# Moving eight column units of the key/value modulation from beside the projections to beside layer 0's attention

## The chip, the cores and the metric

One core of one Trainium2 chip runs the whole program. The metric is the device time of one execution in microseconds. Five engines each run their own instruction list in order: PE (TensorE, matrix products), DVE (VectorE), ACT (ScalarE), POOL (GpSimd) and SP (SyncE), which here only issues the loads of the weights. They meet through semaphores.

## The reference

A decoder of two layers works on 256 tokens of width 1024. All numbers are 32-bit floats.

```
for layer in (0, 1):
    shift, scale, gate (twice each) = silu(c) @ w_ada[layer] + b_ada[layer]
    u = rmsnorm(h) * (1 + scale_m) + shift_m
    layer 0: mix = forgetting attention(u): q, k, v, log f = u @ w_in_a
             q, k = rmsnorm per head; p = softmax(q k / 8 + cum f_q - cum f_k, causal); mix = (p v) @ w_o_a
    layer 1: shared keys/values from rmsnorm(h), modulated by silu(c) @ w_ada_kv; three-branch attention
    h = h + gate_m * mix
    u = rmsnorm(h) * (1 + scale_f) + shift_f
    h = h + gate_f * (64 routed experts, top 8 of them per token, + one shared expert)(u)
```

Two parts matter here. Layer 0's projection has 12 units of 256 columns: four of queries, four of keys, four of values. The modulation vectors are products of one row, silu(c), with wide matrices. Vectors 2 to 7 (gate, and the shift, scale and gate of the feed-forward part of layer 0, and shift and scale of the key/value side) are the ones that the change touches.

## The kernel before

**The ring.** Every weight comes to the core as a unit of 1 MB. One list, `ring_order`, says in which order the units are loaded into 14 slots. SP walks it (L1397): unit n is issued when unit n - 14 has been used up. The list begins with 8 units of layer 0's first two modulation vectors; then come the 12 projection units, `("qkv", j)`, each followed by `COLS_OF_QKV[j]` column units, 24 in all; then eight later column units and the four units of the output projection, mixed; then the experts of layer 0. Numbered from 0, the last projection unit is unit 41, and the first expert unit is unit 56.

**A column unit** holds 256 output columns of a modulation matrix. PE has nothing to do with it: DVE multiplies it with the row silu(c), in two passes of 1024 elements per partition (`dve_columns`, L614), each of which sums into one column of `vectors`. `dve_vectors(done, 1, ...)` adds the biases once all 24 early units are read.

**The projections.** For each unit PE runs `pe_rows_unit` (L565: 16 products, each with two records in the trace) into one PSUM bank. For the eight query and key units ACT squares the result, DVE forms sums and norms the heads (`dve_head_norm`, L917 to L929), PE turns the normed rows (L1619) and ACT copies them to `qT` and `kT_a`. DVE takes its column units between the norms of unit after unit. The four value units are only copied by ACT (L1908) into `v_a`.

**The attention** of layer 0 has eight batches of four heads and 128 queries: four with 128 keys each (t = 0), then four with 256 (t = 1). For each batch, in order: PE computes logits (`pe_logits`, L692 and L697); DVE adds the mask, takes the maximum and negates it (`mask`, L792 to L796); ACT takes exponents (L775); PE turns the probabilities (`turn`, L716); ACT copies them (L767); PE multiplies with the values (`weigh`, L737); DVE divides (`output`, L803 and L2125). Each engine runs ahead by its own order. PE's for batch b is logits(b + 2), weigh(b - 1), turn(b). DVE's is

```
mask(0); mask(1)
for b in range(len(batches)):
    if beside: beside(b)
    if b + 2 < len(batches): mask(b + 2)
    if b >= 1: output(b - 1)
output(len(batches) - 1)
```

Layer 0 passes no `beside`; layer 1 does.

**After it** PE turns the heads (L474) and runs the output projection; DVE prepares the gate (L640), works out the rotary angles, reads two column units, then waits for the gate row (ACT L655), and then for each of three output units reads two more column units and adds the rows (L899, L901). The norm, the router and the choice of experts follow. SP needs the chosen order (`order_i`, waited for at L1419) to load any expert beyond the first four.

Of the kernel before, what the change touches and what calls it, by code (L numbers as in the profile page):

```python
# [24 lines left out]
ALU = mybir.AluOpType  # L25
ACT = mybir.ActivationFunctionType
# [5 lines left out]
NT = SEQ // P  # L32
# [14 lines left out]
QK_SCALE = DH ** -0.5  # L47
# [52 lines left out]
OF_LAYER = [0, 8]  # L100
# [8 lines left out]

VECTOR_STAGES = [range(0, 2), range(2, 8), range(8, 10), range(10, 12), range(12, VECTORS)]  # L110
COLS_PER_VECTOR = 4
COLS_OF_QKV = [2, 2, 1, 2, 1, 2, 1, 2, 3, 3, 3, 2]
COLS_OF_OUT = [2, 2, 2, 2]
COLS_OF_KV = [2, 2, 2, 1, 1]
COLS_OF_OUT_B = [6, 1, 1]
# [21 lines left out]
def ring_order():  # L137

    early, late, last, mixed = (iter(cols_of(i)) for i in range(1, 5))
    order = [("ada", j) for j in range(ADA_UNITS)]  # L140
    for j in range(12):
        order += [("qkv", j)] + [("cols", next(early)) for _ in range(COLS_OF_QKV[j])]
    for j in range(4):
        order += [("cols", next(late)) for _ in range(COLS_OF_OUT[j])] + [("out_a", j)]
    order += expert_units(0)
    for j in range(3):
        order += [("kv", j)] + [("cols", next(last)) for _ in range(COLS_OF_KV[j])]
    order += [("kv", 3)] + [("cmp", j) for j in range(4)] + [("cols", next(last)) for _ in range(COLS_OF_KV[3])]
    order += [("kv", 4), ("kv", 5)] + [("cmp", j) for j in range(4, 8)]
    order += [("cols", next(last)) for _ in range(COLS_OF_KV[4])]  # L150
    order += [("q", j) for j in range(4)]
    for j in range(3):
        order += [("cols", next(mixed)) for _ in range(COLS_OF_OUT_B[j])] + [("out_b", j)]
    order += [("out_b", 3)]
    return order + expert_units(1)
# [46 lines left out]
def build(nc, a, out):  # L202
    with ExitStack() as ctx:
# [5 lines left out]
        def sem(name):  # L209
            if name not in sems:  # L210
                sems[name] = ctx.enter_context(nc.semaphore(name))
            return sems[name]
# [219 lines left out]
        def bcast(ap, shape):  # L432
            return ap.to_broadcast(shape)


        ROUTING_SEMS = ["router_out", "router_copied", "router_turned", "scores_ready", "mask_ready", "ranks_out", "unranked_ready", "unranked_turned",
                        "unranked_copied", "place_ready", "ranked_out", "order_ready", "over_ready", "ends_out",
                        "items_ready", "items_out", "tables_ready", "shared_act", "shared_hid",
# [116 lines left out]
        def pe_rows_unit(pe_, n, bank, lhs, step_ready=None, between=None):  # L555

            landed(pe_, n)
            w = slot(n)
            for t in range(NT):
                if t and between:  # L560
                    between()
                for k in range(KC):
                    if step_ready and t == 0:
                        step_ready(k)
                    mm = pe_.matmul(PS[:, bank, t * UC:(t + 1) * UC], lhs[:, k, t * P:(t + 1) * P],  # L565
                                    w[:, k, :], start=(k == 0), stop=(k == KC - 1))
            mm.then_inc(unit_done, 1)
# [71 lines left out]
        def dve_gate_diag(done, i):  # L639
            done(done.eng.tensor_tensor(gate_diag, of_halves[:, :].unsqueeze(1).to_broadcast([P, KC, DH]),  # L640
                                        vectors[:, GATES[i], :].unsqueeze(2).to_broadcast([P, KC, DH]), ALU.mult),
                 gate_diag_ready)
# [37 lines left out]
        def pe_logits(pe_, kind, batches, keys, b):  # L680
            br, t, g = batches[b]
            w = width(t)
            if b >= 2:
                pe_.wait_ge(scores_read, BATCHES_FROM[kind] + b - 1)
            if kind == "nsa":
                pe_.wait_ge(sem("rotated_copied"), g + 1)
            o = logit_banks(b).rearrange("p (half pair) w -> p half pair w", half=2)
            for i in range(2):
                pair = 2 * g + i
                for half in range(2):  # L690
                    rows = slice(half * DH, (half + 1) * DH)
                    mm = pe_.matmul(o[:, half, i, 0:w], qT[rows, pair, t * P:(t + 1) * P],  # L692
                                    keys(br, pair)[rows, 0:w], start=True, stop=(kind != "fox"))
                if kind == "fox":
                    for half in range(2):
                        rows = slice(half * DH, (half + 1) * DH)
                        mm = pe_.matmul(o[:, half, i, 0:w], forget_queries[rows, t * P:(t + 1) * P],  # L697
                                        forget_keys[rows, pair, 0:w], start=False, stop=True)
            mm.then_inc(logits_out, 1)
# [119 lines left out]
        def act_table(act, function):  # L819
            act.activation(unused[:, :], eps_col[:, :], function)  # L820
# [754 lines left out]
        def _(pe_):  # L1575
# [35 lines left out]
            def turn_unit(j):  # L1611
# [8 lines left out]
                                           src[:, t, c * P:(c + 1) * P], ident[:, :])  # L1620
                mm.then_inc(sem("fox_turned"), 1)

            for j in range(12):
                if j == 11:
                    pe_.wait_ge(sem("fox_v"), 1)
                elif j >= 3:
                    pe_.wait_ge(sem("fox_normed"), j - 2)
                pe_rows_unit(pe_, AT["qkv", j], j % 3, uT)
                if 1 <= j <= 8:
                    turn_unit(j - 1)  # L1630
                if j == 0:
                    forget_turn()
                elif j == 2:
                    forget_sums()
                elif j == 3:
                    forget_turn_rows()
            pe_.wait_ge(forget_rows, 5)
            pe_.wait_ge(sem("fox_copied"), 8)
            pe_.wait_ge(sem("fox_v"), 4)

            def fox_keys(br, pair):
                return kT_a[:, pair, :]

            for b in range(2):
                pe_logits(pe_, "fox", fox_batches, fox_keys, b)
            pe_attention(pe_, "fox", fox_batches, fox_keys,
                         lambda br, kt, hd: v_a[:, kt, hd, :])
            pe_turn_rows(pe_, u, (heads_read, 8), "fox_o")
# [223 lines left out]
        def _(act):  # L1872
# [33 lines left out]
            for j in range(4):  # L1906
                used_up(act, ("qkv", 8 + j))
                done(act.activation(v_a[:, :, 4 * j:4 * j + 4, 0:DH],  # L1908
                                    PS[:, (8 + j) % 3, :].rearrange("p (t h d) -> p t h d", t=NT, h=4), ACT.Copy),
                     sem("fox_v"))  # L1910
                if j == 0:
                    copy_unit(7)
            act_table(act, ACT.Exp)
            act_attention(done, "fox", fox_batches)
            act_copy_turned(done, uT, "fox_o")
            act.wait_ge(sem("angles"), 2)
# [116 lines left out]
        def _(dve):  # L2033
# [42 lines left out]
            for j in range(12):  # L2076
# [7 lines left out]
                if j < 8:  # L2084
                    if j >= 2:
# [1 line left out]
                    dve_head_norm(done, "foxn", j, j % 3,  # L2087
                                  normed[j % 2].rearrange("p (t h d) -> p t h d", t=NT, h=4),
                                  (gain_qa if j < 4 else gain_ka)[:, :], sem("fox_normed"))
            dve.wait_ge(params, 16 * N_PARAMS)  # L2090
            done(dve.tensor_scalar(gain_qb[:, :], gain_qb[:, :], QK_SCALE, None, ALU.mult))
            dve_vectors(done, 1, [(OF_LAYER[0] + SC_F, 1), (OF_KV + 1, 2)])

            def rope_angles():
                dve.wait_ge(consts, 1)
# [29 lines left out]
                done(dve.tensor_tensor(u[:, t, g * UC:(g + 1) * UC].rearrange("p (i d) -> p i d", i=4), heads,  # L2125
                                       rinv.unsqueeze(2).to_broadcast([P, 4, DH]), ALU.mult), heads_read)

            dve_attention(done, "fox", fox_batches, fox_finish)

            def add_mix(layer, name, beside=None):  # L2130
                dve.wait_ge(gate_ready, 2 * layer + 1)
# [22 lines left out]
                dve_columns(dve, [next(late) for _ in range(COLS_OF_OUT[j])])  # L2154

            dve_gate_diag(done, 0)
            rope_angles()
            columns_of_out(0)
            add_mix(0, "out_a", lambda j: columns_of_out(j + 1))
# [252 lines left out]
```

## Time and profile before

| what | us |
|---|---|
| median of 3 runs | 1393.42 (1393.15 to 1394.42) |
| the profiled execution, its own time | 1396.53 |
| its span, first to last instruction | 1394.8 |
| PE busy, of the span | 1338.6 (96%) |
| DVE busy | 428.8 (31%) |
| DMA, bytes and mean rate | 512.94 MB, 368 GB/s |

The busy shares are means over stages with different limits: layer 0's projections and attention fill the time up to about 160 us, its output projection and routing the time up to about 219 us, its experts the time to about 790 us, then layer 1 in the same order. "PE busy" counts matmul records with modelled ends.

### The profile page before, as it was taken

The numbers are of one execution on the slowest core, as the hardware profiler recorded it, in microseconds if no ns is written. First come the engines' busy times: TensorE is split into PE (matmuls) and PEld (weight loads), VectorE is DVE, ScalarE is ACT, GpSimd is POOL, SyncE is SP. The second block draws the span as 40 slices with busy tenths as digits, with TensorE's granted clock in tenths as the row PEclk, the third lists the DMA queues.
The fourth block names the chain that finished last, engine by engine and source line by source line (L and its number), as shares of the span: only waits on it lengthen the run. The fifth ranks groups of instructions, "written<-read, shape, count | busy, mean of one in ns | idle before, by whom it ended". The sixth has DMA issues, their size and how long they took to land.

```text
span 1394.8 us, 20069 instructions
## 1 busy us (share of the span) xinstructions
PE 1338.6 (96%) x8011; PEld 783.8 (56%) x8011; DVE 428.8 (31%) x969; ACT 268.4 (19%) x534; POOL 32.1 (2%) x82
## 2 busy tenths in 40 slices
PE   5998989999999999999899899899999999999997
PEld 1887865465444444444388788754564444444442
DVE  1799672101111111111183698611111111111111
ACT  2222531110111111011133563410110111111100
POOL 4000000001000000000000000000010000000000
PEclk9999999999999999999999999999999999999999
DMA  9999666999999999999999602579999999999996
GB/s 381 390 421 421 266 247 260 385 421 361 423 420 421 422 421 421 421 421 421 421 417 420 252 1 90 220 307 383 420 362 422 420 421 422 421 421 422 420 421 286
DMA packets 71774, 512.94 MB, mean 368 GB/s; under 512 B 8240, under 2 KB 8448, under 8 KB 9728
## 3 DMA queue, kind: packets, MB, share of 16 engines
q1 hardware_dynamic: 70560, 509.64, 88.6%
q0 software_dynamic: 832, 1.39, 0.5%
q8 instruction: 65, 1.06, 0.3%
q10 hardware_dynamic: 288, 0.61, 0.1%
q14 instruction: 29, 0.24, 0.0%
HBM read 510.55 MB, written 1.05 MB: 367 GB/s over the span
## 4 chain that ended last, share of the span: by engine, by line
PE 80%; DMA 8%; DVE 7%; ACT 2%; issue 2%; SPq 1%; DVEq 0%; ACTq 0%
PE PS L987 24%; PE PS L977 13%; PE PS L995 12%; PE PS L1011 11%; PE PS L565 6%; DMA ring<-in_w_in_a_units 4%; DMA ring<-in_w_exp 4%; DVE ring L614 2%; PE PS L737 2%; PE PS L1023 2%; SPq L1397 1%; PE PS L692 1%; PE PS L1852 1%; PE PS L1032 1%; PE PS L716 1%
## 5 line engine op out<-in xcount | busy, mean ns | idle before, releaser
L987 PE MATMUL PS<-ring,scratch 128*32 128x512 f32 (+2 forms) x2176 | 353.7, 593 | 6.7 <-DMA ring<-in_w_exp 5.3
L987 PEld LDWEIGHTS PS<-ring,scratch 128*32 128x32 f32 (+2 forms) x2176 | 111.0, 122 | 242.3 <-issue 240.6
L1342 DVE TENSOR_TENSOR scratch<-PS,gate_row 128x512 f32<-128x512 f32 x100 | 69.2, 692 | 462.3 <-PE PS L995 462.3
L977 PEld LDWEIGHTS PS<-scratch,u 128*128 128x128 f32 x1600 | 186.2, 194 | 38.4 <-issue 36.5
L977 PE MATMUL PS<-scratch,u 128*128 128x128 f32 x1600 | 195.4, 281 | 1.4 <-ACT scratch L1206 1.4
L995 PE MATMUL PS<-ring,scratch 128*32 128x512 f32 (+2 forms) x1088 | 182.2, 596 | 3.4 <-DMA ring<-in_w_exp 2.2
L1011 PE MATMUL PS<-scratch 128*128 128x512 f32 x384 | 172.7, 592 | 0.0
L565 PE MATMUL PS<-ring,uT 128*128 128x256 f32 x672 | 148.6, 380 | 3.6 <-DMA ring<-in_w_in_a_units 3.4
L1214 ACT ACTIVATE scratch<-PS 128x256 f32<-128x256 f32 x50 | 19.2, 384 | 672.9 <-PE PS L987 672.9
L565 PEld LDWEIGHTS PS<-ring,uT 128*128 128x128 f32 x672 | 126.3, 190 | 22.6 <-issue 4.2
L1330 DVE TENSOR_TENSOR scratch<-scratch,PS 128x256 f32<-128x256 f32 x50 | 21.1, 422 | 329.7 <-ACT scratch L1214 329.7
L995 PEld LDWEIGHTS PS<-ring,scratch 128*32 128x32 f32 (+2 forms) x1088 | 52.8, 122 | 123.3 <-issue 121.6
L614 DVE SCALAR_TENSOR_TENSOR ring<-ring,cond_row 128x1024 f32<-128x1024 f32 x96 | 111.8, 1220 | 4.8 <-ACT gate_row L655 3.9
L1011 PEld LDWEIGHTS PS<-scratch 128*128 128x128 f32 x384 | 69.2, 190 | 68.9 <-issue 68.9
L1206 ACT ACTIVATE scratch<-PS 128x512 f32<-128x512 f32 x100 | 59.7, 597 | 145.7 <-PE PS L977 145.7
L737 PE MATMUL PS<-scratch,uT 128*128 128x65 f32 x288 | 37.0, 279 | 4.7 <-ACT uT L767 4.4
L737 PEld LDWEIGHTS PS<-scratch,uT 128*128 128x128 f32 x288 | 34.6, 195 | 9.1 <-issue 6.4
L775 ACT ACTIVATE scratch<-scratch,stats 128x128 f32<-128x128 f32 (+1 forms) x96 | 35.6, 444 | 11.9 <-DVE stats L796 11.9
L1219 ACT ACTIVATE scratch<-PS 128x512 f32<-128x512 f32 x50 | 29.6, 592 | 2.7 <-PE PS L1005 2.7
L565 PE MATMUL PS<-ring,u 128*128 128x256 f32 x128 | 28.7, 381 | 0.0
L1023 PE MATMUL PS<-uT,ring 128*128 128x256 f32 x128 | 28.3, 379 | 0.0
L1023 PEld LDWEIGHTS PS<-uT,ring 128*128 128x128 f32 x128 | 24.3, 190 | 5.0 <-issue 1.9
(346 smaller groups left out, 856.9 us busy)
## 6 DMA issues: line engine op xcount, KB each, us to landing
ring<-in_w_exp SPq DMA_DIRECT2D x384, 1024.0 KB, 16.4
ring<-in_w_ada_columns SPq DMA_DIRECT2D x48, 1024.0 KB, 25.6
ring<-in_w_in_a_units SPq DMA_DIRECT2D x12, 1024.0 KB, 27.5
ring<-in_w_ada_units SPq DMA_DIRECT2D x8, 1024.0 KB, 16.1
ring<-in_w_cmp_units SPq DMA_DIRECT2D x8, 1024.0 KB, 24.0
ring<-in_w_sh_units SPq DMA_DIRECT2D x6, 1024.0 KB, 13.7
ring<-in_w_kv_b_units SPq DMA_DIRECT2D x6, 1024.0 KB, 22.4
ring<-in_w_o_a_units SPq DMA_DIRECT2D x4, 1024.0 KB, 26.4
```

The costliest lines, as they stand in the source:

```text
L565: mm = pe_.matmul(PS[:, bank, t * UC:(t + 1) * UC], lhs[:, k, t * P:(t + 1) * P], w[:, k, :], start=(k == 0), stop=(k == KC - 1))
L614: ins = dve.scalar_tensor_tensor(out=w[:, c, :], in0=w[:, c, :], scalar=1.0, in1=cond_row[:, :], op0=ALU.mult, op1=ALU.mult, accum_out=vec ...
L737: mm = pe_.matmul(PS[:, heads_bank(kind, b), hd * (DH + 1):(hd + 1) * (DH + 1)], pT[:, n * P:(n + 1) * P], values(br, kt, 4 * g + hd), sta ...
L775: eng.activation(p, p, ACT.Exp, bias=stats[:, b % 3, 4 + i:5 + i]).then_inc(probs_ready, 1)
L977: mm = pe_.matmul(PS[:, bank, i * w:(i + 1) * w], u[:, t, k * P:(k + 1) * P], hot[:, t, :], start=(t == 0), stop=(t == NT - 1))
L987: mm = pe_.matmul(PS[places, GU, :], x[:, kk, places], gate_and_up, start=(kk == 0), stop=(kk == KC - 1))
L995: mm = pe_.matmul(PS[places, Y0 + half, :], hT[:, j, places], down[:, j, half * 512:(half + 1) * 512], start=(j == 0), stop=(j == 1))
L1011: mm = pe_.matmul(OUT[t][:, half * 512:(half + 1) * 512], hot_wT[0:rows, t * P:(t + 1) * P], y_rows[0:rows, half * 512:(half + 1) * 512], ...
L1023: mm = pe_.matmul(PS[:, GATHER, i * SEQ:(i + 1) * SEQ], slot(AT[unit])[:, k, i * P:(i + 1) * P], uT[:, k, :], start=(k == 0), stop=(k == K ...
L1206: act.activation(x_pair[g % 2][:, 4 * half:4 * half + 4, :].rearrange("p k s -> p (k s)"), PS[:, gather_bank(g, half), :], ACT.Copy).then_ ...
L1219: act.activation(turned_sb[g % 2], PS[:, GU, :], ACT.Copy).then_inc(group_sem["turned_copied"], 1)
L1342: dve.tensor_tensor(y_rows[:, half * 512:(half + 1) * 512], PS[:, Y0 + half, :], gate_row[:, half * 512:(half + 1) * 512], ALU.mult).then_ ...
```

## The change

Eight of the 24 early column units leave the projections and go behind the last projection unit in the ring; DVE reads one of them at the start of each attention batch, ahead of `mask(b + 2)` (`columns_of_fox`, handed over as `beside`). The last projection unit becomes unit 34 of the ring. `dve_vectors(done, 1, ...)` moves behind the attention, and the scaling of `gain_qb` behind the gate's preparation. On PE the logits of batch 0 are issued ahead of the last value unit, those of batch 1 behind it; the value units go to banks 2, 6, 7, 6 so that the logits' banks 0 and 1 are free, with the waits that this needs. ACT loads its table for exponents ahead of the last value copy instead of behind it.

```diff
--- before.py
+++ after.py
@@ -109,7 +109,8 @@
 
 VECTOR_STAGES = [range(0, 2), range(2, 8), range(8, 10), range(10, 12), range(12, VECTORS)]
 COLS_PER_VECTOR = 4
-COLS_OF_QKV = [2, 2, 1, 2, 1, 2, 1, 2, 3, 3, 3, 2]
+COLS_OF_QKV = [2, 2, 1, 1, 1, 1, 1, 1, 1, 2, 2, 1]
+COLS_BESIDE_FOX = 8
 COLS_OF_OUT = [2, 2, 2, 2]
 COLS_OF_KV = [2, 2, 2, 1, 1]
 COLS_OF_OUT_B = [6, 1, 1]
@@ -140,6 +141,7 @@
     order = [("ada", j) for j in range(ADA_UNITS)]
     for j in range(12):
         order += [("qkv", j)] + [("cols", next(early)) for _ in range(COLS_OF_QKV[j])]
+    order += [("cols", next(early)) for _ in range(COLS_BESIDE_FOX)]
     for j in range(4):
         order += [("cols", next(late)) for _ in range(COLS_OF_OUT[j])] + [("out_a", j)]
     order += expert_units(0)
@@ -433,6 +435,7 @@
             return ap.to_broadcast(shape)
 
 
+        V_BANK = [2, 6, 7, 6]
         ROUTING_SEMS = ["router_out", "router_copied", "router_turned", "scores_ready", "mask_ready", "ranks_out", "unranked_ready", "unranked_turned",
                         "unranked_copied", "place_ready", "ranked_out", "order_ready", "over_ready", "ends_out",
                         "items_ready", "items_out", "tables_ready", "shared_act", "shared_hid",
@@ -1620,12 +1623,20 @@
                                            src[:, t, c * P:(c + 1) * P], ident[:, :])
                 mm.then_inc(sem("fox_turned"), 1)
 
+            def fox_keys(br, pair):
+                return kT_a[:, pair, :]
+
             for j in range(12):
-                if j == 11:
-                    pe_.wait_ge(sem("fox_v"), 1)
-                elif j >= 3:
+                if j == 9:
+                    pe_.wait_ge(forget_rows, 5)
+                elif j == 11:
+                    pe_.wait_ge(sem("fox_copied"), 8)
+                    pe_.wait_ge(sem("fox_normed"), 8)
+                    pe_logits(pe_, "fox", fox_batches, fox_keys, 0)
+                    pe_.wait_ge(sem("fox_v"), 2)
+                elif 3 <= j <= 8:
                     pe_.wait_ge(sem("fox_normed"), j - 2)
-                pe_rows_unit(pe_, AT["qkv", j], j % 3, uT)
+                pe_rows_unit(pe_, AT["qkv", j], V_BANK[j - 8] if j >= 8 else j % 3, uT)
                 if 1 <= j <= 8:
                     turn_unit(j - 1)
                 if j == 0:
@@ -1634,15 +1645,8 @@
                     forget_sums()
                 elif j == 3:
                     forget_turn_rows()
-            pe_.wait_ge(forget_rows, 5)
-            pe_.wait_ge(sem("fox_copied"), 8)
+            pe_logits(pe_, "fox", fox_batches, fox_keys, 1)
             pe_.wait_ge(sem("fox_v"), 4)
-
-            def fox_keys(br, pair):
-                return kT_a[:, pair, :]
-
-            for b in range(2):
-                pe_logits(pe_, "fox", fox_batches, fox_keys, b)
             pe_attention(pe_, "fox", fox_batches, fox_keys,
                          lambda br, kt, hd: v_a[:, kt, hd, :])
             pe_turn_rows(pe_, u, (heads_read, 8), "fox_o")
@@ -1906,11 +1910,12 @@
             for j in range(4):
                 used_up(act, ("qkv", 8 + j))
                 done(act.activation(v_a[:, :, 4 * j:4 * j + 4, 0:DH],
-                                    PS[:, (8 + j) % 3, :].rearrange("p (t h d) -> p t h d", t=NT, h=4), ACT.Copy),
+                                    PS[:, V_BANK[j], :].rearrange("p (t h d) -> p t h d", t=NT, h=4), ACT.Copy),
                      sem("fox_v"))
                 if j == 0:
                     copy_unit(7)
-            act_table(act, ACT.Exp)
+                elif j == 2:
+                    act_table(act, ACT.Exp)
             act_attention(done, "fox", fox_batches)
             act_copy_turned(done, uT, "fox_o")
             act.wait_ge(sem("angles"), 2)
@@ -2087,9 +2092,8 @@
                     dve_head_norm(done, "foxn", j, j % 3,
                                   normed[j % 2].rearrange("p (t h d) -> p t h d", t=NT, h=4),
                                   (gain_qa if j < 4 else gain_ka)[:, :], sem("fox_normed"))
-            dve.wait_ge(params, 16 * N_PARAMS)
-            done(dve.tensor_scalar(gain_qb[:, :], gain_qb[:, :], QK_SCALE, None, ALU.mult))
-            dve_vectors(done, 1, [(OF_LAYER[0] + SC_F, 1), (OF_KV + 1, 2)])
+            def columns_of_fox(b):
+                dve_columns(dve, [next(early) for _ in range(COLS_BESIDE_FOX // len(fox_batches))])
 
             def rope_angles():
                 dve.wait_ge(consts, 1)
@@ -2125,7 +2129,8 @@
                 done(dve.tensor_tensor(u[:, t, g * UC:(g + 1) * UC].rearrange("p (i d) -> p i d", i=4), heads,
                                        rinv.unsqueeze(2).to_broadcast([P, 4, DH]), ALU.mult), heads_read)
 
-            dve_attention(done, "fox", fox_batches, fox_finish)
+            dve_attention(done, "fox", fox_batches, fox_finish, columns_of_fox)
+            dve_vectors(done, 1, [(OF_LAYER[0] + SC_F, 1), (OF_KV + 1, 2)])
 
             def add_mix(layer, name, beside=None):
                 dve.wait_ge(gate_ready, 2 * layer + 1)
@@ -2154,6 +2159,8 @@
                 dve_columns(dve, [next(late) for _ in range(COLS_OF_OUT[j])])
 
             dve_gate_diag(done, 0)
+            dve.wait_ge(params, 16 * N_PARAMS)
+            done(dve.tensor_scalar(gain_qb[:, :], gain_qb[:, :], QK_SCALE, None, ALU.mult))
             rope_angles()
             columns_of_out(0)
             add_mix(0, "out_a", lambda j: columns_of_out(j + 1))
```

## Rows read from the trace of the kernel before

**Rows 1.** The page, the span in 40 equal slices of 34.87 us, clock and DMA in tenths.
```profile
PEclk9999999999999999999999999999999999999999
DMA  9999666999999999999999602579999999999996
```

**Rows 2.** Timeline, PE, the last projection units: start, us, engine, operation, idle before.
```profile
103.56 13.98 PE L565 MATMUL PS<-ring,uT 128*128 128x256 f32 x64
...
119.39 7.14 PE L565 MATMUL PS<-ring,uT 128*128 128x256 f32 x32 [1.85 <-DMA ring<-in_w_in_a_units]
```

**Rows 3.** Busy time by windows: window, length, each engine, clock, DMA share, GB/s.
```profile
90.00:98.00 8.00, 8.00 (x41) 7.05 (x40) 7.39 (x16) 1.40 (x3) 0.00 (x0) 1.00 1.01 421
...
128.00:160.00 32.00, 29.46 (x266) 25.04 (x263) 21.37 (x41) 18.94 (x46) 0.00 (x0) 1.00 0.90 373
```

**Rows 4.** Timeline, DVE: first passes of two column units that follow each other.
```profile
101.97 1.22 DVE L614 SCALAR_TENSOR_TENSOR ring<-ring,cond_row 128x1024 f32<-128x1024 f32 x1
...
104.27 1.22 DVE L614 SCALAR_TENSOR_TENSOR ring<-ring,cond_row 128x1024 f32<-128x1024 f32 x1
```

**Rows 5.** Timeline of the attention's start, PE, DVE and ACT.
```profile
127.38 0.49 PE L692 MATMUL PS<-scratch 64*128 64x128 f32 x4 [0.84 <-ACT scratch L1908]
...
128.34 0.42 PE L692 MATMUL PS<-scratch 64*128 64x128 f32 x4
...
128.64 0.69 DVE L792 TENSOR_TENSOR scratch<-PS,causal 128x512 f32<-128x512 f32 x1 [0.63 <-PE PS L697]
...
130.29 0.69 DVE L792 TENSOR_TENSOR scratch<-PS,causal 128x512 f32<-128x512 f32 x1
130.29 1.28 ACT L775 ACTIVATE scratch<-scratch,stats 128x128 f32<-128x128 f32 x4 [1.55 <-DVE stats L796]
```

**Rows 6.** Timeline, DVE: one mask with t = 1, one output, the next mask.
```profile
137.33 1.22 DVE L792 TENSOR_TENSOR scratch<-PS,causal 128x1024 f32<-128x1024 f32 x1 [1.45 <-PE PS L697]
...
140.05 0.18 DVE L803 RECIPROCAL stats<-PS 128x4 f32<-128x4 f32 x1
...
140.74 1.22 DVE L792 TENSOR_TENSOR scratch<-PS,causal 128x1024 f32<-128x1024 f32 x1
```

**Rows 7.** Timeline, from the last batch's turning to the gate row.
```profile
156.03 1.04 PE L716 MATMUL PS<-ident,scratch 128*128 128x128 f32 x8
...
156.68 1.09 ACT L767 ACTIVATE uT<-PS 128x512 f32<-128x512 f32 x2 [2.10 <-PE PS L716]
157.42 1.97 PE L737 MATMUL PS<-scratch,uT 128*128 128x65 f32 x16 [0.34 <-ACT uT L767]
...
159.71 0.42 DVE L2125 TENSOR_TENSOR u<-PS,stats 128x256 f32<-128x256 f32 x1
160.17 0.69 DVE L640 TENSOR_TENSOR scratch<-of_halves,vectors 128x512 f32<-128x512 f32 x1
160.19 3.60 PE L474 MATMUL PS<-ident,u 128*128 128x128 f32 x16 [0.80 <-DVE u L2125]
...
164.35 1.23 DVE L614 SCALAR_TENSOR_TENSOR ring<-ring,cond_row 128x1024 f32<-128x1024 f32 x1
...
172.92 1.22 DVE L614 SCALAR_TENSOR_TENSOR ring<-ring,cond_row 128x1024 f32<-128x1024 f32 x1 [3.89 <-ACT gate_row L655]
```

**Rows 8.** Windows of 4 us, columns as in Rows 3: where the clock fell, and where not.
```profile
160.00:164.00 4.00, 3.81 (x18) 3.79 (x19) 3.45 (x17) 1.91 (x4) 0.00 (x0) 0.57 0.02 4
...
208.00:212.00 4.00, 3.55 (x21) 3.23 (x21) 2.87 (x12) 0.83 (x2) 0.00 (x0) 0.50 0.00 0
...
844.00:848.00 4.00, 2.80 (x26) 2.59 (x25) 3.77 (x7) 2.62 (x7) 0.00 (x0) 1.00 0.00 0
```

**Rows 9.** A window in the routing, SP's wait for the order, SP's next load.
```profile
204.00:208.00 4.00, 1.27 (x9) 0.59 (x6) 2.35 (x11) 3.92 (x4) 0.00 (x0) 0.99 0.00 0
...
SPq L1419 <- DVE order_i L1301: 56.4, 2, 29.1
...
219.81 1.34 SPq L1397 DMA_DIRECT2D ring<-in_w_exp  x2
```

## The prediction

> **What bounds the kernel now.** I read four views in this order.
>
> First the slices of the page [rows 1]. They show that the DMA engines are full nearly throughout, but fall to 6 tenths in slices 5 to 7 (139 to 244 us) and to nothing around slice 24. A pause of the DMA is where something other than the weights sets the time. The edits fall into slices 1 to 5, up to the first pause.
>
> Second the timeline of PE through the projections [rows 2]. The reader is to see that the units follow without a gap: units 9 and 10 of the projection together take 103.56 to 117.54, 6.99 each, and only unit 11 waits, 1.85 us, for its weights. The window from 90 to 98 us says the same, PE 8.00 of 8.00 while DVE has 7.39 and the DMA runs at 421 GB/s [rows 3]. So two things run nearly level here, but PE is the one that sets the pace, with 1.85 us of DMA on top at the end.
>
> Third the attention, 128 to 160 us. PE is busy for 29.46 us of 32, DVE for 21.37 [rows 3]. DVE has 10.63 us free. The chain of waits goes around from PE to DVE to ACT and back; DVE waits for PE in most batches (1.45 us before the mask that starts at 137.33 [rows 6]).
>
> Fourth what follows. After the attention DVE is done with its first two late column units about 4 us before the gate row comes (it idles 3.89 us [rows 7]), and from there the routing is a plain chain. In the routing the DMA moves nothing, and SP stands at L1419 for the order of the experts, 29.1 us at the longest; its next load goes out at 219.81 [rows 9]. A shift of the attention's end is therefore a shift of the routing, of that load and of all that comes after. Nothing behind it has slack that would absorb it: the loads that the chosen order gates cannot start sooner, and PE starts on the experts from the same routing.
>
> **The change, part by part.**
>
> *Fewer column units among the projections.* Seven fewer stand ahead of projection unit 11 in the ring (41 becomes 34). A unit of 1.049 MB at 421 GB/s takes 2.49 us [rows 3], so its weights come up to 17 us sooner. But only the wait can be saved: 1.85 us. PE cannot start unit 11 before unit 10 ends, 117.54 [rows 2]. DVE's free time in that stretch buys nothing, as PE had no gap to close. The waits before the second and third unit stay, as the column units ahead of those are the same.
>
> *Logits of batch 0 ahead of unit 11.* One batch of them takes 0.96 us of PE (127.38 to 128.34 [rows 5]). Queries and keys are complete by then: unit 8 and the last turn are over at 103.56 [rows 2], and the last key copy follows directly. Unit 11 then starts at 118.50 and ends at 118.50 + 7.14 = 125.64 (before: 119.39 + 7.14 = 126.53). That is 0.89 us sooner.
>
> *The start of the attention.* Before, the first mask starts 1.26 us after the first logits (127.38 to 128.64) and the second at 130.29, so a mask with t = 0 takes 1.65 us [rows 5]. In the changed kernel mask(0) is done while unit 11 runs. Logits 1 need no value copy and can start at 125.64, so mask(1) starts at 125.64 + 1.26 = 126.90, where it was 130.29: 3.39 us sooner. Exponents 0 (1.28 us of ACT [rows 5]) still stand behind the copy of the last values in ACT's queue, which costs nothing, since DVE is what is late next (below).
>
> *Eight column units beside the batches.* This is the big term. Two column units that follow each other start 2.30 us apart (101.97 and 104.27 [rows 4]), so eight cost DVE 18.4 us. None of them can be read during unit 11: `beside(0)` stands behind mask(1), and mask(1) waits for logits that come after unit 11. DVE's list from mask(1) to the end:
>
> - masks with t = 0: number 1, 2 and 3, 3 x 1.65 = 4.95 us;
> - masks with t = 1: four, each 2.72 us (137.33 to 140.05 [rows 6]), 10.88 us;
> - outputs: seven at 0.69 us (140.05 to 140.74 [rows 6]), and the last at 0.60, 5.43 us;
> - column units: 18.4 us.
>
> The sum is 39.66 us. Before, the same stretch lasted from 130.29 to 160.13 [rows 5, 7], 29.84 us, and held 21.26 us of DVE work. So the columns use up 8.6 us of idle time and 9.82 us are left over. Could DVE still wait inside? PE was busy for 29.46 us with all eight batches [rows 3]; one with t = 1 is at most twice one with t = 0, so at most 4.9 us, while DVE needs 2.30 + 2.72 + 0.69 = 5.71. PE runs ahead. At the tail, mask(7) ends near 159.2. Its exponents take at most twice the 1.28 us of 128 keys [rows 5], and from its turning to the end of its weighing it was 3.36 us (156.03 to 159.39 [rows 7]): 165.1. DVE comes to the last output at 165.9. So I take no idle time. Attention ends at 126.90 + 39.66 = 166.56 instead of 160.13: **+6.43 us**.
>
> *Work put behind the attention.* The three vector instructions of `dve_vectors` and the scaling of `gain_qb` now stand there. DVE did the gate's preparation and 16 small instructions in 164.35 - 160.17 = 4.18 us [rows 7]; without the 0.72 or so of the first, whose row has 0.69, that is 0.22 us each, so four cost 0.87 us. They lie inside the idle 3.89 us ahead of the gate row: 0. Without that cover they would cost 0.9. The gate product of PE waits for about 0.7 us of them, but stands behind a whole output unit of some 7 us.
>
> *The queue of SP.* The eight units are numbers 36 to 43, and free the slots of 50 to 57. With batches of 4 to 5.7 us, the last output unit (55) is issued when batch 5 has read number 41, near 156 us, and lands well ahead of its use, which is behind three other units' products. The first two expert units (56, 57) go out near 161 and 164, where they went out by about 130; the ten behind them follow the late columns, as before. All twelve have until about 225 us, and the DMA is empty from some 200 us on (0.00 in 204 to 208 [rows 9]). Two loads later by 30 us are 5 us of DMA time moved into that gap: 0. Without the gap they would cost those 5 us.
>
> *Sum:* -3.39 + 9.82 + 0 + 0 = +6.43 us on the profiled execution (span 1394.8, own time 1396.53). Its own time stands 3.1 us above the median; I put the difference on the median: 1393.42 + 6.43 = **1399.9 us**, +0.46%.
>
> **Bounds.** TensorE's clock is the unknown. At the attention's end it is granted at 0.57 between 160 and 164 us and 0.50 between 208 and 212 [rows 8], so at 1.2 GHz in part or whole, and the turning of the heads took 3.60 us [rows 7]. If the new timing kept it at 2.4 GHz there, turning would take half (-1.8 us) and the second spot might give the same again: the lower bound is 6.43 - 3.6 = +2.8. If the lower level instead lasts on into the first output unit, up to half of that unit's 7.14 us doubles: +3.6, upper bound +10. Between them I keep the middle, as the clock fell before at a tail like the one expected.
>
> The Trainium skill ("TensorE: Matmul & The Clock Gate", section "What's actually happening") says that the throttled state is the default and that activity releases it. That rule speaks against this change, as it thins PE out: by it the next rival would be likelier. The trace agrees only in part, for the window of 844 to 848 had PE busy for 2.80 us of 4 at a clock of 1.00 [rows 8].
>
> **Rivals.**
>
> *The lower clock takes the attention.* PE's share falls from 29.46/32 = 0.92 to about 29.46/40 = 0.74 in the attention. If the clock went to 1.2 GHz, a batch would need up to 2 x 4.9 = 9.8 us of PE where DVE needs 5.71, 4.1 us more; two or three such batches give +8.2 to +12.3 us on top: 1408 to 1412 us. For it: the fall at 160 us. Against it: layer 1's attention, which shows 0.70 (2.80 of 4) beside a DVE at 3.77, keeps 1.00 there [rows 8]. Chance 0.10.
>
> *The shift is hidden.* If the weights' stream set the end by itself, the time of the routing would not matter, and the result is 1393.4, at most 0.9 less. For it: the DMA stands at 9 tenths in most slices [rows 1]. Against: it is empty for some 20 us before 219.81, and SP waits for the routing there [rows 9]. Chance 0.05.
>
> *Faster: the columns fit in the gaps.* If the column passes ran only in DVE's idle time, the attention would keep its pace and end 3.4 us sooner: 1390.0 us. It is decided by the price of one unit: the list has 21.26 us besides the columns and 166.56 becomes 160.13 when eight cost 160.13 - 126.90 - 21.26 = 11.97 us, 1.50 us each. Below 1.50 it is a gain, and at 1.07 the whole 3.4 (8.58 us of idle time by eight). The row has 2.30 [rows 4]; the passes touch only SBUF and have the same operands. Chance 0.05.
>
> **How the numbers follow.** DVE-bound attention, 1396.2 to 1403.5: 0.80. The rivals: 0.10, 0.05, 0.05. The likeliest is 1399.9. The range of 1396.2 to 1404 leaves out the rivals, 0.20 together. 0.2% is 2.8 us, about what a measurement can tell from no change. Faster by more than that: 0.05. Within it: the hidden shift and the lowest edge of the main case, 0.07. Slower: 0.88.
>
> **What the profile would show.** Unit 11 without a wait, its last record near 125.6; the second mask near 126.9; DVE without idle time between the masks, at 4.6 and 5.7 us per batch, where PE and ACT wait for it; the last output near 166.6; SP's load behind the routing near 226.2; and all later stages of the same length. A DVE that idles in the attention, a clock under 1.00 before 160 us, or a routing that does not shift would make the prediction wrong. So would a column pass that is not 1.22 us beside ACT and PE at work on the same PSUM and scratch.

## The result, and the profile after

The changed kernel takes 1407.2 us (median of 9 runs, 1401.19 to 1419.07), the kernel before 1394.42 (9 runs, 1391.8 to 1402.75). The ratio is 1.0094, 95% interval 1.0072 to 1.0116: slower by about 13 us, where 6.4 were forecast, and over the upper end of the forecast range (1404). The profiled execution of the changed kernel is its slowest run (1419.07 us, span 1417.3), so of its trace the places count, and the medians for the size.

The page, clock and DMA in 40 slices of 35.4 us (before: [rows 1]):

```profile
PEclk9999697999999999999999988999999999999999
DMA  9999474899999999999999700759999999999996
```

The clock has new holes in slices 5 and 7 and in slices 24 and 25. The last two lie in layer 1 (815 to 886 us), which the change does not touch.

Timeline of the changed kernel, from the last value unit on (before: [rows 2] and [rows 5]; L565 is now L568, L792 L795, L614 L617):

```profile
118.14 7.17 PE L568 MATMUL PS<-ring,uT 128*128 128x256 f32 x32
...
126.52 0.69 DVE L795 TENSOR_TENSOR scratch<-PS,causal 128x512 f32<-128x512 f32 x1 [6.65 <-PE PS L700]
...
128.17 1.23 DVE L617 SCALAR_TENSOR_TENSOR ring<-ring,cond_row 128x1024 f32<-128x1024 f32 x1
...
136.73 1.23 DVE L617 SCALAR_TENSOR_TENSOR ring<-ring,cond_row 128x1024 f32<-128x1024 f32 x1
...
142.41 1.22 DVE L617 SCALAR_TENSOR_TENSOR ring<-ring,cond_row 128x1024 f32<-128x1024 f32 x1
```

Unit 11 starts without a wait and is over at 125.3. The second mask starts at 126.52 (forecast: 126.90; the places of one and the same work differ by up to 0.9 us between profiled executions, so this gap says nothing). From there DVE shows no idle time, and a batch with 256 keys takes it 142.41 - 136.73 = 5.68 us (forecast: 5.71). Up to here the arithmetic held.

The same timeline, the tail (before: [rows 7]):

```profile
158.88 1.91 PE L719 MATMUL PS<-ident,scratch 128*128 128x128 f32 x8
...
161.12 3.65 PE L740 MATMUL PS<-scratch,uT 128*128 128x65 f32 x16 [0.34 <-ACT uT L770]
164.56 1.91 PE L719 MATMUL PS<-ident,scratch 128*128 128x128 f32 x8
...
165.03 0.42 DVE L2129 TENSOR_TENSOR u<-PS,stats 128x256 f32<-128x256 f32 x1
...
166.40 3.65 PE L740 MATMUL PS<-scratch,uT 128*128 128x65 f32 x16
...
170.16 0.18 DVE L806 RECIPROCAL stats<-PS 128x4 f32<-128x4 f32 x1 [4.71 <-PE PS L740]
...
170.85 3.68 PE L477 MATMUL PS<-ident,u 128*128 128x128 f32 x16 [0.80 <-DVE u L2129]
```

DVE has done output 6 by 165.45 and then waits 4.71 us for PE. Weighing takes PE 3.65 us where it took 1.97 before, and turning 1.91 instead of 1.04 [rows 7]. Two weighings and one turning stand in a row there: PE's list has the weighing of batch 6 ahead of the turning of batch 7. The attention ends at 170.79, not at 166.56.

Windows of 4 us of the changed kernel (columns as in [rows 3]):

```profile
140.00:144.00 4.00, 2.00 (x16) 1.46 (x16) 3.83 (x8) 2.19 (x5) 0.00 (x0) 1.00 0.91 348
144.00:148.00 4.00, 3.93 (x22) 3.46 (x24) 3.86 (x7) 0.58 (x2) 0.00 (x0) 0.60 0.58 190
...
152.00:156.00 4.00, 1.16 (x9) 0.95 (x8) 3.86 (x7) 2.67 (x6) 0.00 (x0) 0.88 0.56 231
156.00:160.00 4.00, 4.00 (x21) 4.00 (x21) 3.83 (x8) 1.21 (x3) 0.00 (x0) 0.50 0.68 238
...
168.00:172.00 4.00, 3.20 (x16) 3.01 (x16) 1.67 (x6) 0.00 (x0) 0.00 (x0) 0.50 0.24 102
...
224.00:228.00 4.00, 4.00 (x20) 3.42 (x20) 0.22 (x1) 0.60 (x1) 0.00 (x0) 0.50 0.01 2
```

PE has 2.00 of 4 us to do, then 1.16 of 4, while DVE is full; after each of them the clock is lower, and from 156 to 172 us it stands at 1.2 GHz.

How the shift grows along the program, in the two profiled executions, each number the start in the changed kernel less that before: turning of the heads 170.85 - 160.19 = 10.7 us; SP's first load of a chosen expert 231.48 - 219.81 = 11.7; SP's first load of the shared expert, deep in layer 0's experts, 288.53 - 272.70 = 15.8; the same load in layer 1, 988.63 - 966.25 = 22.4. The step from 11.7 to 15.8 has the lower clock beside it: it stood at 0.50 from 220 to 236 us in the changed kernel, over the end of the routing and the first expert products, and at 1.00 from 216 us on in the kernel before. The last step, 6.6 us, falls in layer 1, where the clock of this one execution was down for longer (slices 24 and 25).

### The profile page after: what moved, and what is told of

Same layout as the page of the kernel before. It is cut to its first block, busy times and chain, and to the rows that moved or that the text cites. A ratio compares the mean times of both kernels' runs of the same rounds, so it can differ in the third digit from the quotient of the medians.

```text
span 1417.3 us, 20074 instructions
## 1 busy us (share of the span) xinstructions
PE 1358.9 (96%) x8011; PEld 800.6 (56%) x8011; DVE 429.3 (30%) x969; ACT 268.3 (19%) x534; POOL 32.1 (2%) x82
## 3 DMA queue, kind: packets, MB, share of 16 engines
HBM read 510.55 MB, written 1.05 MB: 361 GB/s over the span
## 4 chain that ended last, share of the span: by engine, by line
PE 83%; DMA 6%; DVE 6%; ACT 2%; issue 1%; SPq 1%; DVEq 0%; ACTq 0%
PE PS L990 24%; PE PS L980 13%; PE PS L998 12%; PE PS L1014 11%; PE PS L568 10%; DMA ring<-in_w_exp 4%; DMA ring<-in_w_in_a_units 2%; PE PS L1026 2%; DVE ring L617 2%; PE PS L740 2%; SPq L1400 1%; PE PS L1856 1%; PE PS L1035 1%; PE PS L719 1%; DVE stats L798 1%
## 5 line engine op out<-in xcount | busy, mean ns | idle before, releaser
L568 PE MATMUL PS<-ring,uT 128*128 128x256 f32 x672 | 149.2, 381 | 1.2 <-DMA ring<-in_w_in_a_units 0.9
L568 PEld LDWEIGHTS PS<-ring,uT 128*128 128x128 f32 x672 | 126.8, 191 | 20.1 <-issue 1.9
L617 DVE SCALAR_TENSOR_TENSOR ring<-ring,cond_row 128x1024 f32<-128x1024 f32 x96 | 112.3, 1221 | 4.6 <-ACT gate_row L658 3.7
L740 PE MATMUL PS<-scratch,uT 128*128 128x65 f32 x288 | 44.0, 312 | 10.1 <-ACT uT L770 9.8
L740 PEld LDWEIGHTS PS<-scratch,uT 128*128 128x128 f32 x288 | 41.5, 227 | 15.1 <-issue 12.8
L568 PE MATMUL PS<-ring,u 128*128 128x256 f32 x128 | 28.7, 381 | 0.0
## 6 DMA issues: line engine op xcount, KB each, us to landing
ring<-in_w_kv_b_units SPq DMA_DIRECT2D x6, 1024.0 KB, 22.4
```

The lines of the kernel that those rows point to most:

```text
L617: ins = dve.scalar_tensor_tensor(out=w[:, c, :], in0=w[:, c, :], scalar=1.0, in1=cond_row[:, :], op0=ALU.mult, op1=ALU.mult, accum_out=vec ...
L740: mm = pe_.matmul(PS[:, heads_bank(kind, b), hd * (DH + 1):(hd + 1) * (DH + 1)], pT[:, n * P:(n + 1) * P], values(br, kt, 4 * g + hd), sta ...
```

## The experiments

Each is compared with the kernel before, run beside it in three groups (e1 to e4: median 1394.02; e5 to e8: 1393.94; e9 to e11: 1395.2; beside the changed kernel it had 1394.42). So times of different groups compare to about 1 us. "First shared load" is SP's first `w_sh` load in layer 0, a landmark free of layer 1; the kernel before has it at 272.70 us.

**e1: fill PE's idle time in the attention.** On the changed kernel:

```diff
+        BUSY_BEFORE_FOX_HEADS = {2: 4, 3: 8, 4: 8, 5: 8, 6: 8, 7: 8}
...
+                elif kind == "fox" and b in BUSY_BEFORE_FOX_HEADS:
+                    pe_keep_busy(pe_, BUSY_BEFORE_FOX_HEADS[b], heads_bank(kind, b), slice(4 * (DH + 1), 512 - P))
```

> The changed kernel with matrix products of no use put ahead of the weighing of the attention's batches 2 to 7 on PE (4, then 8 each, into unread columns of the heads' bank), so that PE does not fall idle there. Theory 1 (the excess over my forecast is TensorE's lower clock in the attention, its tail and what follows): the clock stays at 1.00 from 140 to 175 us, the last output comes near 166.5 us instead of 170.8, the output unit after it starts some 5 us sooner, and the median falls from 1407 to 1399 to 1401, with less spread. Theory 2 (the excess is DVE's or the ring's, or lies in layer 1): no change, 1405 to 1409, or slower by the added PE work.

Measured: 1401.59 us (12 runs, eleven of them 1400.59 to 1403.18), ratio 1.0049 (1.0032 to 1.0066). The clock is 1.00 through the attention, and turning the heads takes 1.97 us. The attention ends at 168.9, the first shared load comes at 278.39, 5.7 us after that of before. The chain that ended last shows why the end is not at 166.5 (start, us, what; L883 is the filling):

```profile
159.99 2.05 PE PS L883 x16
162.04 1.74 PE PS L742 x16
163.77 0.88 PE PS L719 x8
164.66 1.78 PE PS L883 x16
166.44 1.75 PE PS L742 x16
```

In the tail the filling stands in the chain itself, some 2 us. Even so the median is 5.6 us under that of the changed kernel, with more work to do. Theory 2 is out.

**e2: the columns alone.** The kernel before with the ring's order, `columns_of_fox` and the place of `dve_vectors` of the change, and nothing on PE or ACT:

```diff
+COLS_OF_QKV = [2, 2, 1, 1, 1, 1, 1, 1, 1, 2, 2, 1]
+COLS_BESIDE_FOX = 8
...
-            dve_attention(done, "fox", fox_batches, fox_finish)
+            dve_attention(done, "fox", fox_batches, fox_finish, columns_of_fox)
```

> The kernel before with the column units moved alone: PE, ACT and the banks as before, no logits ahead of the last value unit. Theory 1 (DVE sets the attention's pace, and the clock falls with it): the attention starts 1.8 us sooner than before, mask(1) near 128.5 us, so it ends some 2 us later than in the changed kernel; 1408 to 1411. Theory 2 (the harm comes from the reordered PE work, not from the columns): 1393 to 1396.

Measured: 1408.22 us (6 runs), ratio 1.0075 (1.005 to 1.0101). The turning of the heads starts at 172.70, 1.9 us after that of the changed kernel. The columns do the harm.

**e3: the first logits alone.** The changed kernel with `COLS_OF_QKV` as before and none beside the attention.

> The changed kernel with all 24 early column units beside the projections as before, so only the logits of batch 0, the banks, the table load and the place of the vector work are changed. Theory 1: DVE is full to 127.2 us with columns, so mask(0) comes at 127.2 instead of 128.6 and the gain is 1 to 1.5 us: 1392 to 1393.5. Theory 2 (the reordering itself does harm): above 1396.

Measured: 1393.87 us (12 runs), ratio 0.9992 (0.9972 to 1.0011). The turning starts at 158.67 (before 160.19), the first shared load at 271.77: about 1 us, as Theory 1 has it, and too small for the medians (1393.87 is just over its range).

**e4: two column units, in the tail.** The changed kernel with

```diff
+COLS_OF_QKV = [2, 2, 1, 2, 1, 2, 1, 2, 3, 3, 2, 1]
+COLS_BESIDE_FOX = [0, 0, 0, 0, 0, 0, 1, 1]
```

> The changed kernel with 22 column units beside the projections and only two beside the attention, at batches 6 and 7, where DVE of the kernel before waited 1.8 to 2.6 us for PE at each output. Theory 1 (columns cost only where DVE has no idle time left): the wait for unit 11 is gone, DVE is free for mask(0) at 123, no cost at the tail; attention ends near 157, 3 us sooner than before, and the clock falls no earlier than it did: 1389.5 to 1391.5. Theory 2 (any column unit in the attention thins PE out and costs the clock): 1396 or more.

Measured: 1394.91 us (12 runs, 1391.19 to 1400.48), ratio 1.0004 (0.9982 to 1.0027). The turning starts at 157.09 and the first shared load comes at 269.53, 3.2 us ahead of before, as expected; the median shows none of it. Four of the twelve runs are at 1400, with mean clocks of 0.983 to 0.985, while the fastest has 0.993. The places were predicted right and the time was not.

**e5: less filling, none in the tail.** As e1, with `{2: 4, 3: 6, 4: 6, 5: 6}`.

> The changed kernel with fewer of the idle-filling products than in the run with them ahead of batches 2 to 7: only ahead of the weighing of batches 2 to 5 (4, 6, 6, 6), none in the tail, where they delayed the last output by about 2.4 us. Theory 1 (my term of +6.4 us for DVE is right, the rest is the clock): the clock is 1.00 up to 158 us, the last output ends at 166 to 167 us, and the median is 1399.5 to 1400.5, 6 us over the kernel before. Theory 2 (the column units cost more than DVE's time): the last output stays at 168.5 or later and the median at 1401.5 or more.

Measured: 1411.7 us (5 runs, 1409.02 to 1413.07), ratio 1.012 (1.0093 to 1.0146). Theory 1 missed. The numbers of Theory 2 hold, but not its cause: DVE is done at 165.7 as forecast, and the last output's reciprocal starts at 169.00 after 3.33 us of waiting for PE. The clock was 0.88 from 160 to 164 us and 0.50 from there to 172. The filling that ended with batch 5 left the tail to the lower clock. Why the five runs lie 4.5 us above those of the changed kernel is not shown: the profiled one turns the heads at 169.70, sooner than the changed kernel, and it falls a further 3.9 us behind the kernel before only between 683 and 723 us, where layer 1 begins.

**e6: no column passes.** The changed kernel with the eight units waited for and freed, and two elements copied in place of the two passes.

> The changed kernel without the two passes over each of the eight column units beside the attention: DVE waits for the unit, copies two elements and frees the slot, so vectors 6 and 7 hold other values (key/value side of layer 1). It shows what the passes alone cost. Theory 1: DVE has 18 us less, the attention runs at the pace of PE and ACT as before, the clock stays up to its tail, and the last output ends near 157 us instead of 170.8; SP issues the first chosen expert near 217 us instead of 231.5; median 1389 to 1392. Theory 2 (the ring's order or the waits of PE do the harm): the attention still ends after 160.

Since vectors 6 and 7 feed layer 1, its median (1490.08 us) tells nothing; up to the end of layer 0 the trace can be read. The turning of the heads starts at 156.59 and takes 1.97 us; the first expert product comes at 213.47, where it came at 218.68 before and 232.07 in the changed kernel; the clock is 1.00 in every window from 118 to 200 us. The last output is where Theory 1 put it, and the first chosen load comes at 214.61, sooner than the 217 expected. The ring's order and PE's new waits cost nothing.

**e7: the kernel before with filling alone.** Ahead of the weighing of batches 6 and 7 one product each, three ahead of the turning, two in the routing:

```diff
+            pe_keep_busy(pe_, 3, 7, slice(4 * (DH + 1), 512 - P))
             pe_turn_rows(pe_, u, (heads_read, 8), "fox_o")
...
+            pe_keep_busy(pe_, 2, 7)
             pe_.wait_ge(routing["mask_ready"], layer + 1)
```

> The kernel before with idle-filling products alone: one ahead of the weighing of batches 6 and 7, three ahead of the turning of the heads, two of 512 columns in the routing ahead of the wait for the mask of chosen experts, where PE idles 2.7 us. Theory 1 (the clock is worth microseconds in the kernel before too, and its spread from 1391 to 1405 is the clock): turning takes 2.0 us instead of 3.6, the gather in the routing 2.0 instead of 3.6, 3 us less: 1390.5 to 1392, and fewer runs above 1398. Theory 2: no difference, since the clock falls elsewhere or by chance.

Measured: 1390.93 us (12 runs, 1389.24 to 1396.84), ratio 0.998 (0.9964 to 0.9995). Its timeline on PE:

```profile
159.75 1.97 PE L474 MATMUL PS<-ident,u 128*128 128x128 f32 x16
...
209.38 2.02 PE L980 MATMUL PS<-scratch,u 128*128 128x128 f32 x16
```

The turning took 3.60 before [rows 7]. The first shared load comes 3.2 us sooner. So the kernel before loses some 3 us to the clock too, and e7 does not get all of it back: its clock fell in another place of the routing (below, at e11).

**e8: e4 with the filling of e7.**

> The version with the first logits ahead and only two column units beside the attention, in its tail, with the same idle-filling products as in the run on the kernel before. Its attention ended 3.1 us sooner but its runs split between 1392 and 1400 us. Theory 1 (the split is the clock in the tail and the routing): 1387.5 to 1389.5 and fewer runs near 1400. Theory 2 (the split comes from layer 1, which nothing here touches): the low runs fall by 2 to 3 us, the share of high ones stays.

Measured: 1387.69 us (12 runs, 1385.37 to 1394.94), ratio 0.9952 (0.9934 to 0.9971): faster than both kernels. The turning starts at 156.53, the first expert product at 210.70, the first shared load at 264.73, 8.0 us ahead of before. Nine of the twelve runs are under 1390; the others, up to 1394.94, have mean clocks of 0.989 to 0.993.

**e9: filling in measure.** As e1, with `{2: 4, 3: 8, 4: 8, 5: 8, 6: 4, 7: 3}`.

> The changed kernel with idle-filling products ahead of the weighing of batches 2 to 7 (4, 8, 8, 8, then only 4 and 3 in the tail, where eight each had stood in the chain themselves). Theory 1 (DVE's list is the +6.4 us and the clock the rest): the clock stays at 1.00 to the end of the attention, the last output ends at 166.5 to 167.5 us instead of 168.9, and the median is 1399 to 1401. Theory 2 (the tail falls to the lower clock with so few): last output at 169 or later, median over 1404.

Measured: 1406.19 us (11 runs, 1401.55 to 1414.31), ratio 1.0074 (1.0048 to 1.0099). In the profiled execution the clock fell again, and the last output waited 4.92 us for PE, as Theory 2 had it. Five of the runs, up to 1403.05, lie where those of e1 do, the other six at 1406.19 and above. So e9 cannot tell how long DVE alone is, and e11 was made to.

**e10: four column units, batches 4 to 7.** As e4, with

```diff
+COLS_OF_QKV = [2, 2, 1, 2, 1, 2, 1, 1, 2, 2, 2, 2]
+COLS_BESIDE_FOX = [0, 0, 0, 0, 1, 1, 1, 1]
```

> First logits ahead, 20 column units beside the projections, four beside the attention, at batches 4 to 7. DVE's list after the first logits is 39.66 - 9.2 = 30.5 us. Theory 1 (the columns cost only what exceeds DVE's idle time): last output ends at 157.0 to 157.6 us, as with two units (157.0), median 1393 to 1395.5. Theory 2 (each unit costs in proportion, 1.2 us or so): the last output ends near 160, median 1397 or more.

Measured: 1402.62 us (12 runs, 1395.25 to 1407.81), ratio 1.0051 (1.0027 to 1.0076). Timeline:

```profile
158.62 0.18 DVE L806 RECIPROCAL stats<-PS 128x4 f32<-128x4 f32 x1
163.82 0.18 DVE L806 RECIPROCAL stats<-PS 128x4 f32<-128x4 f32 x1 [4.57 <-PE PS L740]
```

Output 6 comes at 158.62, later than the whole attention should have ended. Two things that the expectation left out bring it there: the second mask starts at 128.04, not at 126.9, and DVE still waits 1.56 us for PE before the mask that starts at 135.19, ahead of its first column unit, time that the units behind it cannot use. DVE's sum over the stage was too coarse. The last output then waits 4.57 us at the lower clock (0.50 in 156 to 168). Half the columns cost 7.4 us, where all of them cost 12.8. Theory 1 is out; Theory 2 has the median in its open range, but the last output, at 164.5, not near 160, and not the cause.

**e11: the changed kernel with the clock held.** The filling of e9, and three products ahead of the turning and two in the routing as in e7.

> The changed kernel with the even filling of the attention, three products ahead of the turning of the heads and two in the routing, the same as in the run on the kernel before that gave 1390.93. With the clock held in both, the difference is the change without the clock. Theory 1: DVE's list, +6.4 us, and up to 1 us of filling: 1397 to 1398.5. Theory 2 (the columns cost more than DVE's time, or the ring is late): 1400 or more.

Measured: 1397.27 us (12 runs, 1395.97 to 1398.4). Against e7, the kernel before with the same two fillings behind the attention, that is +6.34 us; their first shared loads, 276.15 and 269.53, are 6.62 apart. Timeline and two windows:

```profile
161.88 2.00 PE L742 MATMUL PS<-scratch,uT 128*128 128x65 f32 x16 [0.39 <-ACT uT L773]
...
165.26 1.90 PE L742 MATMUL PS<-scratch,uT 128*128 128x65 f32 x16
...
167.27 0.18 DVE L809 RECIPROCAL stats<-PS 128x4 f32<-128x4 f32 x1 [1.05 <-PE PS L742]
```

```profile
160.00:164.00 4.00, 3.28 (x27) 3.09 (x28) 3.90 (x8) 2.31 (x6) 0.00 (x0) 1.00 0.50 158
164.00:168.00 4.00, 3.92 (x36) 3.73 (x34) 2.84 (x9) 1.09 (x2) 0.00 (x0) 1.00 0.88 313
```

The attention ends at 167.9, 1.05 us of it a wait for PE. Its runs spread over 2.4 us, those of the changed kernel over 18.

The two landmarks are not a clean price of DVE's work. The attention of e11 ends at 167.90 and that of e7 at 159.69, 8.2 us apart. Of these, 1.05 are the wait for PE, and 0.85 stand in e11's trace before its attention begins (its first mask starts at 119.11, that of the changed kernel, with the same instructions up to there, at 118.25), which leaves 6.3. The shift is 1.6 us smaller behind the routing because e7's clock fell there, and its router products took 3.80 us where those of e11 took 2.22. Window and timeline of e7, then timeline of e11:

```profile
196.00:200.00 4.00, 3.71 (x23) 2.74 (x21) 2.84 (x7) 1.94 (x4) 0.00 (x0) 0.65 0.11 44
...
197.06 3.80 PE L534 MATMUL PS<-uT,scratch 128*64 128x256 f32 x16 [0.29 <-DMA scratch<-in_w_router_rows]
...
205.26 2.22 PE L537 MATMUL PS<-uT,scratch 128*64 128x256 f32 x16 [0.29 <-DMA scratch<-in_w_router_rows]
```

## Why the prediction was wrong

**The direction and the DVE sum were right.** DVE sets the pace of the changed attention, gap-free, at the forecast period. From the second mask on it has 39.5 us of work (126.52 to 165.45, and the last output), and the sum gave 39.66. With most of the clock's falls filled on both sides the change costs 6.34 us (e11 less e7), and the sum gave 6.43. That these two agree to 0.1 us is luck: each against the kernel before of its own group they are 5.1 us apart, and in the traces a wait for PE, a later start and e7's slower router products happen to cancel. That the weights' wait before unit 11 was all there was to win among the projections, that the ring has room, and that the routing carries the shift on, held too (e3, e6, the landmarks).

**The step that failed is the bound on TensorE's clock.** The prediction took the fall at the tail to be the same in both kernels ("Between them I keep the middle, as the clock fell before at a tail like the one expected"), took no idle time for DVE at the last output, put the clock's possible cost at +3.6 us at most, in the output unit alone, and gave the clock inside the attention a chance of 0.10. It is worth 1407.2 - 1397.3 = 9.9 us in the changed kernel (e11) and 1394.0 - 1390.9 = 3.1 us in the one before (e7). The difference, 6.8 us, stands beside the 6.34 of DVE, and together they are 13.1 where 12.8 were measured. Taken each against its own group the shares are 7.7 and 5.1. Both splits have to add up, being made of the same medians, so the sum is no test of its own; what shows the cause is that products of no use on PE alone took 9.9 us away. The prediction had named the signs: the clock was under 1.00 before 160 us (0.60 from 144 to 148), DVE waited 4.71 us, and SP's load behind the routing came at 231.48, not 226.2.

**Where it goes.** Not where the rival had it. Inside the batches the lower clock is hidden, as DVE is slower still: its period stays 5.68 us with PE at 1.2 GHz. The cost comes where DVE's masks run out, and one weighing, one turning and another weighing follow each other at 3.65, 1.91 and 3.65 us: the attention ends 4.2 us after its forecast in the profiled execution. The tail estimate had the last batch's steps without the batch ahead in PE's queue, and at the full clock; even with the clock held, the last output waits 1.05 us (e11, with 0.83 us of filling in it). More comes at the end of the routing and in the first expert products: the shift grows from 11.7 to 15.8 us between the first chosen load and the first shared one in the profiled executions. That the attention's thinner load also makes the later falls more frequent was not shown: e7 and e11 changed both places together.

**The rule against the change was weighed too low.** The Trainium skill ("TensorE: Matmul & The Clock Gate", "What's actually happening") has it that activity releases the throttle. The prediction set one window of layer 1 against it, PE busy 2.80 of 4 us at 1.00 [rows 8]. The changed kernel comes to 2.00 and 1.16 of 4, and there the trace agrees with the rule. The mean share that the prediction used (0.74) hid those windows. The busy share of one window does not decide it, though: in the kernel before PE was busy for 2.15 of 4 us from 116 to 120, and the clock stayed at 1.00 there and after.

**The rival "faster"** is out at the price in its own condition: a unit costs 2.30 us as before. It holds in part for two units in the tail (e4, e8), where DVE had idle time of that size.

## What to carry to other kernels

Work that is put beside a stage paced by round trips between engines costs first what exceeds its engine's idle time, batch by batch and in the order of the queue, and second what it takes from TensorE's load; here the second was about as large as the first. So count the other engine's period, then look at PE's busy share in the emptiest windows, as a warning and not as a rule, and price the tail at 1.2 GHz. Column work goes where DVE waits for PE anyhow, and short idle gaps on PE ahead of critical products are worth filling with products of no use, if the filling ends before the wait does.

## What the hardware showed that I had not expected

The clock's fall is not settled by the instructions alone. e9 and e11 have the same instructions up to the turning of the heads, and PE was busy 3.23 and 3.32 of 4 us from 156 to 160; then e9's clock went to 0.84 and 0.50 from 160 to 168 us, and e11's stayed at 1.00. This window of e9 stands against the first of e11 above:

```profile
160.00:164.00 4.00, 3.37 (x22) 3.19 (x23) 3.90 (x8) 2.21 (x6) 0.00 (x0) 0.84 0.43 127
```

Most of the spread between runs goes with this clock. The kernel before ran in 1391.38 us at a mean clock of 0.996 and in 1405.34 at 0.985: 14.0 us. An estimate from these means: lower by 0.011 over 1395 us is 31 us at 1.2 GHz instead of 2.4, and half of these 31 us is 15. The changed kernel has 1401.19 at 0.988 and 1419.07 at 0.975, 17.9 us for what by the same sum would be 18. The mean alone does not give a run's time: the changed kernel has both 1401.19 and 1406.79 at 0.988, and e5 has 1409.02 at 0.990. Products of no use, up to 2 us of them per batch, made the changed kernel faster (e1, e11), but too few of them did not (e5, 1411.7 us).
